# Two blocks of transformer layers: both expert layers gather their rows, and the relay of down columns works in quads and runs on through gates and mixers

## The reference

```
q = (xt @ w_q).reshape(T, 8, 2, 128)                  # T = 256 tokens, 8 heads, two halves
s1 = einsum('thd,hnd->thn', q[:, :, 0], sub_keys[0])   # 128 keys per half
s2 = einsum('thd,hnd->thn', q[:, :, 1], sub_keys[1])
v1, i1 = top_k(s1, 16);  v2, i2 = top_k(s2, 16)
cand = v1[..., :, None] + v2[..., None, :]             # 256 candidates
best, pos = top_k(cand, 16)
expert = take_along_axis(i1 * 128 + i2, pos)           # 16 of 16384 experts, per token and head
gate = softmax(best)
a = einsum('td,ted->te', x, w_down[expert])            # 128 experts per token
y = einsum('te,ted->td', gelu(a) * gate, w_up[expert])
```

## Time and profile before

| | |
|---|---|
| median of 3 runs | 3121.55 us (3118.06 to 3126.91) |
| profiled execution, whole | 3136.85 us |
| its span, first to last instruction | 3135.1 us |
| mean granted clock of TensorE | 0.933 |
| busy, of the span | TensorE 87%, VectorE 64%, ScalarE 42%, GpSimd 34% |
| DMA | 773.94 MB, mean 247 GB/s |
| of it GpSimd's queue | 411.91 MB |
| of it SyncE's queue | 360.75 MB |
| stages | feed-forward to 205; stick-breaking mixer; feed-forward 381 to 568; gate; feed-forward 627 to 805; pool mixer; feed-forward 880 to 1064; gate and latent attention to 1235; expert layer 0 to 2159; sparse attention to 2321; expert layer 1 to 3119 us |

### The profile page before, as it was taken

How to read it: one execution, slowest core, us unless ns; L and a number is a source line. 1 busy time by engine, 2 the same in 40 slices (tenths; PEclk the granted TensorE clock), 3 DMA queues, 4 the chain that set the end, 5 groups by cost and what they waited for, 6 DMA issues and landing times.

```text
span 3135.1 us, 44731 instructions
## 1 busy us (share of the span) xinstructions
PE 2725.9 (87%) x14826; PEld 2204.2 (70%) x14826; DVE 2011.3 (64%) x3647; ACT 1305.2 (42%) x2197; POOL 1073.1 (34%) x1355
## 2 busy tenths in 40 slices
PE   8998799899899978999997699998965787777776
PEld 8986699799789866999996578887753333333222
DVE  6665467576566655577779955555857666666654
ACT  4446444444444454544447645544542222212111
POOL 4422344144144200000005500000006777777774
PEclk9999899999999988999998899998987888999888
DMA  9973399699589742555551055555428999999996
GB/s 343 372 255 123 108 361 366 206 340 376 187 313 377 241 160 77 173 183 184 181 181 54 0 178 192 193 193 180 167 80 335 371 356 383 363 373 355 372 363 259
DMA packets 217334, 773.94 MB, mean 247 GB/s; under 512 B 29600, under 2 KB 29600, under 8 KB 216336
## 3 DMA queue, kind: packets, MB, share of 16 engines
q0 software_dynamic: 118192, 411.91, 35.1%
q1 hardware_dynamic: 99040, 360.75, 33.6%
HBM read 704.39 MB, written 68.16 MB: 246 GB/s over the span
## 4 chain that ended last, share of the span: by engine, by line
PE 52%; POOL 11%; DVE 6%; issue 6%; DMA 4%; ACT 2%; DVEq 0%; ACTq 0%; POOLq 0%; SPq 0%
PE ps L1508 15%; PE ps L1509 14%; PE ps L1510 14%; POOL arena L398 6%; PE ps L1876 6%; POOL arena L394 5%; DMA arena<-down_rows,arena 3%; DVE first_hot L1451 1%; PE ps L1656 1%; PE ps L1554 1%; DVE arena L1382 1%; DVE second_hot L1454 1%; DVE arena L1463 1%; DVE w_lo L903 0%; ACT arena L537 0%
## 5 line engine op out<-in xcount | busy, mean ns | idle before, releaser
L903 DVE TENSOR_TENSOR w_lo<-raw,w_hi 128x1024 fp32r<-128x1024 f32 x681 | 831.6, 1224 | 644.0 <-ACT w_hi L502 639.0
L502 ACT ACTIVATE w_hi<-raw 128x1024 fp32r<-128x1024 f32 x681 | 719.1, 1056 | 650.0 <-PE ps L1510 430.0
L1508 PE MATMUL ps<-act_hi,w_hi 128*128 128x256 f32 x2728 | 780.6, 286 | 40.3 <-DVE w_lo L903 21.1
L1509 PE MATMUL ps<-act_lo,w_hi 128*128 128x256 f32 x2728 | 774.4, 284 | 0.0
L1510 PE MATMUL ps<-act_hi,w_lo 128*128 128x256 f32 x2728 | 774.3, 284 | 0.0
L1876 PE MATMUL ps<-arena 128*128 128x512 f32 x1024 | 522.1, 669 | 177.3 <-ACT arena L655 177.3
L1508 PEld LDWEIGHTS ps<-act_hi,w_hi 128*128 128x128 f32 x2728 | 525.8, 193 | 49.5 <-issue 28.6
L1876 PEld LDWEIGHTS ps<-arena 128*128 128x128 f32 x1024 | 214.7, 215 | 473.7 <-issue 257.6
L1509 PEld LDWEIGHTS ps<-act_lo,w_hi 128*128 128x128 f32 x2728 | 526.1, 193 | 5.6 <-issue 2.4
L1510 PEld LDWEIGHTS ps<-act_hi,w_lo 128*128 128x128 f32 x2728 | 525.8, 193 | 0.0
L1382 DVE SCALAR_TENSOR_TENSOR arena<-arena 128x1024 f32<-128x1024 f32 x256 | 313.9, 1227 | 258.2 <-DMA arena<-down_rows,arena 257.2
(11 more groups left out here) (243 smaller groups left out, 3033.6 us busy)
## 6 DMA issues: line engine op xcount, KB each, us to landing
raw<-in_stream SPq DMA_DIRECT2D x684, 512.0 KB, 3.4
arena<-in_stream POOLq DMA_DIRECT2D x128, 512.0 KB, 8.7
down_rows<-arena POOLq DMA_DIRECT2D x512, 128.0 KB, 5.8
pad<-in_ln POOLq DMA_DIRECT2D x4, 1024.0 KB, 6.4
arena<-down_rows,arena POOLq DMA_INDIRECT x256, 6.2
arena<-in_stream,arena POOLq DMA_INDIRECT x256, 6.3
arena<-in_subkeys POOLq DMA_DIRECT2D x2, 1024.0 KB, 5.9
x<-in_x SPq DMA_DIRECT2D x1, 1024.0 KB, 5.1
```

The source lines that it names most:

```text
L502: act.activation(w_hi[:, u % SPLIT, :], raw[:, u % RAW, :], ACT.Copy).then_inc(hi_done, 1)
L903: dve.tensor_tensor(w_lo[:, u % RAW, :], raw[:, u % RAW, :], w_hi[:, u % SPLIT, :].bitcast(F32), ALU.subtract).then_inc(lo_done, 1)
L1508: pe.matmul(dst, lhs[0], rhs[0], start=first, stop=False, **kw)
L1509: pe.matmul(dst, lhs[0], rhs[1], start=False, stop=False, **kw)
```

## The change

Both expert layers run the code of expert layer 1. `gather`, `gathered` and `rows_gathered` take the layer as an argument; the dense path, its one-hot matrices and its semaphores go. The stream's down and up units are no longer loaded by SyncE for layer 0 either: it jumps from the query units of layer 0 to the sparse attention.

The relay now has 256 tiles. A tile is no longer a unit, but a quarter (32 partitions) of each of four consecutive units; four tiles make a quad, whose transposes together give rows of 4 KB. A quad is stored in four DMAs of 512 KB, each from all 128 partitions. There are four phases with buffers of their own: the first feed-forward block; q, k, v of the first mixer; then everything from the second feed-forward block to the last gate, without a break; and the projections of the latent attention. GpSimd's wait for all stores now stands after the first block, before stick-breaking, after the last gate, and once in the latent attention. The transposes are spread over the splits of gates and mixers as well.

In the gather, the ring of down rows has 8 slots, and GpSimd waits once before each four picks, for dots and uses together. Queries are kept in 4 slots in place of 16. At item 13 of layer 0 four units of the next mixer are split ahead.

```
-RELAY_IN, RELAY_OUT = 6, 6
-RELAY_PLAN = [2] + [2, 1] * 9 + [1, 2] + [0]
+N_MAIN = DOWN[0] + DOWN[1] - AFTER
+QUAD = 4
+RELAY_IN, RELAY_OUT = 6, 3
+RELAY_FFN = [[1] + [2] * 17 + [3] * 3, [3] * 17 + [2] * 4, [3] * 17 + [2] * 4, [3] * 16 + [2] * 5]
+RELAY_GATE = [6, 8]
+RELAY_POOL = 6
+RELAY_QKV = [4, 2, 2]
+RELAY_MLA = [4, 2, 2]
+RELAY_PHASES = [
+    (sum(RELAY_FFN[0]), range(2048, 8192, UNIT), (12288, 16384, 20480)),
+    (sum(RELAY_QKV), (10240, 11264), (12288, 16384)),
+    (sum(sum(f) for f in RELAY_FFN[1:]) + sum(RELAY_GATE) + RELAY_POOL, range(2048, 8192, UNIT), (12288, 16384, 20480)),
+    (sum(RELAY_MLA), (14336, 15360), (22528,)),
+]
-DOWN_RING, UP_RING, DIAG_RING = 6, 12, 8
+ISSUE, Q_KEPT = 4, 4
+DOWN_RING, UP_RING, DIAG_RING = 2 * ISSUE, 3 * ISSUE, 8
...
+            def relay_load(n):
+                slot, at, _, _, _, _ = RELAY[n]
+                unit, a = DOWN[n // NK] + n % NK // QUAD * QUAD, n % QUAD
+                pool.dma_start(area(at, UNIT),
+                               stream[unit:unit + QUAD, 32 * a:32 * a + 32, :]).then_inc(relay_in[slot], 16)
+            def relay(count, phase):
+                ahead = len(RELAY_PHASES[phase][1])
+                for n in range(relayed[0], relayed[0] + count):
+                    pool.wait_ge(relay_turned, n + 1)
+                    if n + ahead < RELAY_START[phase + 1]:
+                        relay_load(n + ahead)
+                    if n % QUAD == QUAD - 1:
+                        _, _, _, slot, at, _ = RELAY[n]
+                        row = NK * (n - QUAD + 1)
+                        rows = down_rows[row:row + NK * QUAD].rearrange("(u c r) k -> c u r k", u=QUAD, c=4)
+                        for c in range(4):
+                            pool.dma_start(rows[c], area(at + UNIT * c, UNIT)
+                                           ).then_inc(relay_out[slot], 16)
...
-                        if p >= DOWN_RING:
-                            pool.wait_ge(dot_done, p - DOWN_RING + 1)
-                        pool.indirect_dma_start(down_in[:, p % DOWN_RING, :], None, down_rows[:, :],
-                                                at).then_inc(down_row[p % DOWN_RING], 16)
-                        if p >= UP_RING:
-                            pool.wait_ge(up_used, p - UP_RING + 1)
+                        if p % ISSUE == 0 and p >= DOWN_RING:
+                            pool.wait_ge(dot_done, p - DOWN_RING + ISSUE)
+                        if p % ISSUE == 0 and p >= UP_RING:
+                            pool.wait_ge(up_used, p - UP_RING + ISSUE)
+                        pool.indirect_dma_start(down_in[:, p % DOWN_RING, :], None, down_rows[:, :], at,
+                                                element_offset=NK * NK * D * layer).then_inc(down_row[p % DOWN_RING], 16)
...
+            def relay(count=1):
+                for n in range(relayed[0], relayed[0] + count):
+                    slot, at, filled, out, place, nth = RELAY[n]
+                    dve.wait_ge(relay_in[slot], 16 * filled)
+                    if n % QUAD == 0:
+                        relay_free(out, nth - 1)
+                    dve.transpose(area(place, QUAD * UNIT)
+                                  .rearrange("p (c a k s) -> p a c k s", c=4, a=4, k=KD)[:, n % QUAD],
+                                  area(at, UNIT).rearrange("p (k c r) -> p c k r", k=KD, c=4)).then_inc(relay_turned, 1)
+                relayed[0] += count
...
-                    split(KD)
+                    split_and_relay(KD, RELAY_POOL)
...
-                if i == 1:
-                    rows_gathered()
-                    layer_norm(True)
-                    continue
...
+                rows_gathered(i)
+                layer_norm(PICKS * (i + 1))
```

More of the change, by code:

```diff
@@ L357, in x_changed @@
                 pool.wait_ge(x_ready, t.after(x_ready, TB))
[L359 to L383, removed]
@@ L385, in gather, with relay_begin @@
-            def gather():
+            relayed = [0]
+            def relay_load(n):
[3 more added lines that the diff above has]
+                               stream[unit:unit + QUAD, 32 * a:32 * a + 32, :]).then_inc(relay_in[slot], 16)
+            def relay_begin(phase):
+                for n in range(RELAY_START[phase], RELAY_START[phase] + len(RELAY_PHASES[phase][1])):
+                    relay_load(n)
@@ L414, in _ @@
                 norm()
-                relay(2 * i)
+                if i == 0:
+                    relay_begin(0)
+                    relay(sum(RELAY_FFN[0]), 0)
+                    for s in range(RELAY_OUT):
+                        relay_stored(s, 0)
+                    relay_begin(1)
+                else:
+                    relay(sum(RELAY_FFN[2]), 2)
                 x_changed()
@@ L419, in _ @@
                     pool.dma_start(area(A_STICKC, STICK_COLS), stickc).then_inc(stick_in, 16)
+                    relay(RELAY_QKV[0], 1)
+                    power(32, 64, 32)
+                    relay(RELAY_QKV[1], 1)
+                    power(32, 64, 32)
+                    relay(RELAY_QKV[2], 1)
+                    for s in range(2):
+                        relay_stored(s, 1)
+                    pool.wait_ge(stick_in, t.after(stick_in, 16))
+                    stick_breaking()
                 else:
@@ L681, in gathered @@
                         exp_gates(n + 2)
+                    if n == ITEMS - 3 and layer == 0:
+                        split(SPLIT)
                 diagonals(4 * ITEMS - 1)
@@ L880, in _ @@
-                for j in range(NK % TURN - RING):
-                    split()
-                    chunk_high(NK - NK % TURN + RING + j, j % RING)
-                split(RING)
+                gathered(i)
                 layer_norm()
@@ L1000, in head_norm @@
                                   ALU.add).then_inc(var_ready, 1)
-                split(4)
+                for n in range(4):
+                    split()
+                    if n < relays:
+                        relay()
                 dve.wait_ge(rstd_ready, t.after(rstd_ready))
@@ L1416, in pair @@
-                def pair(n):
-                    take(n)
-                    for j in range(SPREAD):
-                        split()
-                        if j < len(pieces):
-                            pieces[j](n)
-                with t.loop(NK // (PAIRS * SPREAD), [(hi_done, PAIRS * SPREAD), (scores_taken, PAIRS),
-                                                     (dve_step, PAIRS * TOPK_STEPS)]) as n:
-                    for p in range(PAIRS):
-                        pair(n * PAIRS + p)
```

445 lines of the change are left out of this document (105 added, 340 removed).

## The result

The changed kernel takes **3844.6 us** (median of 4 runs, 3835.1 to 3857.8), the one before 3119.8 on the same chip: ratio 1.233, interval 1.228 to 1.238. The forecast was 3265 in a range of 3150 to 3335. The sign was right; the size was 725 us in place of 144.

A forecast was written before the change was run, and what follows sets the result against it. Feed-forward blocks met TensorE and DMA limits at once, the gather its feeding, the dense layer TensorE and VectorE; 3135.1 + 203 - 11 - 10 + 8 - 126 + 80 = 3279 us span; 3265 us median, range 3150 to 3335.

The forecast's parts named there:

- (b): Four feed-forward blocks: doubled relay at 375 GB/s costs +203 us, less 11 us for stores running on under the next norm.
- (e): Both gathers: waits once for four picks cost +40 us a layer, +80 in all, ends 0 and +176.
- (a): Expert layer 0: gathered at layer 1's pace in place of dense, -126 us.
- (c): Ends of the second and third feed-forward blocks: GpSimd's wait for all stores goes, -10 us, perhaps less.
- (d): Relay tiles in gates, mixers and latent attention: mostly hidden, +8 us, bounded by 0 and 30.
- Faster streams: Feed-forward blocks and both gathers: a higher DMA rate wins from 378 GB/s on, median about 3080 us at 385; chance 0.12.
- The clock falls: Feed-forward blocks: TensorE waiting for tiles loses clock; with the gather waits' upper end, 3365 us; chance 0.10.
- Hidden waits: Both gathers: the ring of 8 hides the grouped waits, so +80 us goes, 3185 us; chance 0.20.
- Share 1.0: Confirming sign: feed-forward windows of about 210, 247, 242 and 243 us have the DMA engines at share 1.0.
- 370 to 378 GB/s: Confirming sign: the DMA rate expected in the four feed-forward windows.
- the list of what would be wrong: Blocks under 225 us, gathers under 740 us, or block clock well under 1 with DMA share below 0.95.

The follow-up runs named there:

- e5_all: Changed kernel with relay loads of whole units, stores of 32 partitions in 4 KB rows, and gather waits before every pick; 3245.4 us, ratio 1.026.
- e6_pieces: Changed kernel with per-pick waits and the relay of the kernel before: a tile is a unit, stored in 1 KB pieces; 3227.5 us, ratio 1.021.
- e1_waits: Changed kernel with GpSimd waiting before each gather again, not once for four picks; 3649.0 us, ratio 1.158.
- e4_both: Changed kernel with relay loads of whole units and each store made as four of 32 partitions, grouped waits kept; 3426.1 us, ratio 1.088.
- e8_four: Kernel before with only its relay loads cut into four runs out of four neighbouring units (G = 4); 3250.8 us, ratio 1.039.
- e9_before: The kernel before itself, unchanged, profiled a second time; 3116.5 us.
- e10_eight: Kernel before with only its relay loads cut into eight runs out of eight neighbouring units; 3189.2 us, ratio 1.022.
- e11_sixteen: Kernel before with only its relay loads cut into sixteen runs out of sixteen neighbouring units; 3135.8 us, ratio 1.006.

## Why the prediction was wrong, step by step

**(b) The relay's blocks: the step that failed.** It says "I take 375 GB/s as what the engines give when they always have work" and prices a store by its size, "512 KB from 128 partitions in 4 KB rows". The pattern of the load, four runs out of four units, was given no price at all, and that of the store only by its row length. The price was about 450 us, 335 of them in the blocks by the stages. Without the spread fault (e5_all) the blocks take 221, 250, 248, 246, or +158 us against my +192. Here my rate was off the other way. 376 GB/s at share 1.01 in the earlier trace rows was not a ceiling: TensorE was busy 50.00 of 50 us there, so the block can have moved just what TensorE asked for. With more to move, and the same shapes of transfers (e6_pieces), the same engines give 415 to 416 in 50 us windows.

**(e) The grouped waits: mechanism right, size wrong.** GpSimd's idle time is released by the use of up rows, as forecast, 4.28 and 7.46 us at a time. But I had +40 us a layer, with +88 as the end. Undoing them gives 102 and 98 us in the change (e1_waits), 91 and 82 with the spread repaired (e4_both to e5_all). I had taken TensorE at full clock; it ran at 0.82 to 0.83 in these gathers, as the windows show, and at 0.88 in the earlier trace rows. The loop that I had computed at the measured clock (+1.45 us a group) was the nearer one, and I had set it aside as an end. One reading was loose too: of the 190 us before the gathers that I called nearly all "issue", 151 are that the earlier trace rows; the rest already waited for other engines.

**(a) Layer 0 gathered: right in sign, less in size.** 930 to 836 us with per-pick waits, -94 for -126.

**(c) The waits for stores: right where I looked, and moved.** After the second and third block the norm follows at once. But three of the new phase ends have a wait for stores in the chain:

```profile
275.31 18.97 DMA down_rows<-arena
388.81 19.34 DMA down_rows<-arena
1647.43 20.19 DMA down_rows<-arena
```

They are 59 us, where I had -21 for stores run on and stalls gone. But most of it belongs to the spread: GpSimd stands 17.9 and 20.1 us after its last store at the first and the third of these places, and in e5_all 3.6 and 7.0 us. At the second it stands 16.1 us in e5_all, but the stores had landed 10 us before that ended.

**(d) Gates and mixers:** +8, bounded by 30. In e5_all the stick-breaking, gate and pool stages are within 5 us and the latent attention +15: 22 in all, inside the bounds. In the change itself it is +97, with landings of 10 to 29 us in the chain of these stages.

**The rivals.** *Faster streams* was right on its rate in the blocks (410 to 416 GB/s in their middle in e4_both to e6_pieces) and still did not win: the gathers it counted on stayed at 347 to 357 GB/s. In e5_all GpSimd issues both gathers of a pick in 0.94 + 0.30 us each at best, and 1.10 to 1.13 + 0.3 on the mean. That would make 0.524 MB / 1.42 us = 370 GB/s with no other wait, under the 416 that the engines gave in the blocks. So the issue, not the engines, seems to set the pace; no run tested it. *The clock falls* named a symptom. The granted clock did fall, to 0.81 to 0.88 in the blocks; the Trainium skill (TensorE: Matmul & The Clock Gate, "HAM oscillation") ties such a fall to waits for DMA, and the trace agrees: TensorE is idle for 69 to 122 us of each block's window, where it was busy nearly throughout at clock 1.00 before. But it did not set the time: in e5_all the clock is 0.91 to 0.93 in the last three blocks, and TensorE is still idle for 35 to 40 us of each (190.30 of 225 us busy, 207.26 of 246): it waits for tiles and is not what they wait for. *Hidden waits* was refuted by e1_waits.

**My signs.** "Share 1.0" came true at once (0.99 to 1.04) and would have confirmed the forecast for anyone who read that column alone. "370 to 378 GB/s" did not, and that is the column that told. And the list of what would be wrong had no sign for slower blocks that could fire: a fallen clock counted only with a share below 0.95, and the clock fell to 0.81 with the share at 1.02.

**Does any version win?** None that ran. The best, e6_pieces, is 2.1% slower than before. Its accounts: layer 0 gains 95 us, and a relayed tile in a block that is full costs 1.049 MB / 415 = 2.5 us. Of the 92 tiles added in the blocks some 25 to 30 would have to go elsewhere at no cost just to break even (an estimate, 69 us by 2.5); that was not tried.

**What stays open.** Why, in the bursts, the 4 KB packets of a tile read from 4, 8 or 16 units take some 100 ns longer than those of one contiguous run. Why six loads of G = 4 in flight together are not carried by more engines: they still need 31 to 33 us. How the price in the change divides between these two. And why layer 1 is 13 to 34 us longer in e5_all and e6_pieces than before with the same order of waits; the chips differ too, and e9_before on another chip had 790.

## What to carry to other kernels

Before pricing a moved or re-tiled DMA by its bytes, read its two access patterns as the DMA sees them, and look at the size of the outermost dimension: with 4 there, a load of the same 512 KB landed after 30 us and not 9, and the stores and stream loads beside it landed later too. Then judge a DMA-heavy stage by GB/s and by the count of packets under 512 B, never by the busy share alone, and call a rate a ceiling only if no other engine was full in that window. A wait taken once for a group of four cost 82 to 102 us a layer here; in groups of two, with two more up slots, it cost 18 us and nothing.

## What the runs showed of the hardware

- A GpSimd DMA of 128 rows whose slowest dimension is k (4 or 8) adds (16 - k) x 128 / k packets of 4 bytes: 384 and 128. With 16 it adds none.
- With k = 4 about four of its 4 KB packets are under way at a time, with k = 8 up to eight, with k = 16 up to 16. As the first of six, with no stream load under way, a load of 512 KB lands after 12 us (k = 4), 7 us (k = 8) and 5 us (k = 16, cut into 16 runs), and after 4 us as one contiguous run.
- A 4-byte packet takes 9 ns (median). A 4 KB packet of a load cut into runs from 4, 8 or 16 units took about 275 ns in the bursts above, one of a contiguous load about 170.
- A load with k = 4 or 8 is also dearer to issue: 680 ns (L390 above), 707 in e8_four and 617 in e10_eight, against 541 in e11_sixteen and 555 for the load of the same size in the kernel before:

```profile
L367 POOL DMA_DIRECT2D arena<-in_stream x128 | 70.8, 555 | 0.0
```

- The DMA share can be 1.04 at 282 GB/s and 1.03 at 416 GB/s.
- The slow loads hold up other transfers: SyncE's loads of 512 KB in the blocks, in a queue of their own and unchanged, landed after 10.5 to 11.6 us in the change and 10.2 to 12.3 in e8_four, where they took 6.5 to 6.6. The stores of e8_four, unchanged too, landed after 20.0 us for 5.6.
